# A three-branch mixer in float32 on one core: the next group's key norm, first-group projections and merge gates in other places

## What is computed

```python
def hybrid_mixer(h, w_in, ...):
    p = jnp.einsum('bsd,de->bse', h, w_in)
    u, q, k, v, zr, gl = jnp.split(p, IN_SPLITS, axis=-1)
    y_a = multiscale_pool(u, pool_w, pool_scale)
    y_b = diff_attention(q, k, v, ...)
    y_c = rwkv7_bidir(zr, ...)
    ys = jnp.stack([y_a, y_b, y_c], axis=2)
    branch = jnp.einsum('bsnc,ncd->bsnd', ys, w_branch)
    gates = jax.nn.sigmoid(gl.reshape(b, s, N_BRANCH, D_MODEL) + b_gate)
    merged = jnp.sum(gates * branch, axis=2)
    return jnp.einsum('bsd,de->bse', merged, w_out)

...
    kk = kh * heads(k_k)
    kk = kk / jnp.maximum(jnp.sqrt(jnp.sum(kk * kk, axis=-1, keepdims=True)), 1e-12)
```

## Time and profile before

| | us |
|---|---|
| median of 3 runs | 4690.75 |
| lowest and highest | 4683.18, 4692.92 |
| the profiled execution | 4692.97 |
| its span, first to last instruction | 4691.1 |
| TensorE busy in it | 4439.5 (95%) |
| mean granted clock of TensorE | 0.967 |

### The profile page before, as it was taken

One profiled execution on the slowest core, in us unless ns is written; L12 is line 12 of the kernel. 1 busy time (PEld: TensorE's weight loads), 2 busy tenths in 40 slices (PEclk: granted clock), 3 DMA queues, 4 the chain that ended last, 5 costly groups with the idle time before them and its releaser, 6 DMA issues.

```text
span 4691.1 us, 60760 instructions
## 1 busy us (share of the span) xinstructions
PE 4439.5 (95%) x25140; PEld 2924.7 (62%) x25140; DVE 1411.2 (30%) x3439; ACT 868.6 (19%) x2217; POOL 328.8 (7%) x274
## 2 busy tenths in 40 slices
PE   7999989989998999999998999899999999999999
PEld 3676674434443567675443444587887788788888
DVE  3665550121001556662011000321222331312332
ACT  3123220010000222221001000222222202222220
POOL 0122210000000022120000000000110000011000
PEclk8999989999999999998999999999999999999999
DMA  2001002212221110001221222111111111111111
GB/s 102 33 28 41 32 15 78 84 58 72 76 76 60 53 36 28 33 28 61 81 81 54 76 76 77 45 50 46 55 50 46 50 68 54 48 56 50 51 58 63
DMA packets 71342, 261.60 MB, mean 56 GB/s; under 512 B 7920, under 2 KB 7920, under 8 KB 70816
## 3 DMA queue, kind: packets, MB, share of 16 engines
q1 hardware_dynamic: 69168, 250.62, 15.4%
q10 hardware_dynamic: 1904, 7.11, 0.5%
HBM read 253.51 MB, written 4.19 MB: 55 GB/s over the span
## 4 chain that ended last, share of the span: by engine, by line
PE 88%; DVE 4%; issue 3%; ACT 2%; DVEq 1%; POOLq 0%; DMA 0%; ACTq 0%; SPq 0%
PE ps L2240 26%; PE ps L1422 24%; PE ps L2361 9%; PE ps L1591 4%; PE ps L2326 4%; PE ps L1441 2%; PE ps L1525 2%; PE ps L2270 2%; PE ps L830 1%; PE ps L837 1%; PE ps L796 1%; PE ps L2251 1%; PE ps L822 1%; PE ps L1544 1%; PE ps L2261 1%
## 5 line engine op out<-in xcount | busy, mean ns | idle before, releaser
L2240 PE MATMUL ps<-xT,ring 128*128 128x512 f32 x2656 | 1176.1, 602 | 66.3 <-ACTq L678 47.1
L2240 PEld LDWEIGHTS ps<-xT,ring 128*128 128x128 f32 x2656 | 508.0, 193 | 718.8 <-issue 718.8
L1422 PE MATMUL ps<-xT,ring 128*128 128x264 f32 (+2 forms) x3392 | 800.8, 392 | 17.7 <-DVE arena L1910 10.4
L1422 PEld LDWEIGHTS ps<-xT,ring 128*128 128x128 f32 (+1 forms) x3392 | 643.6, 193 | 138.6 <-DVE arena L1910 13.9
L2361 PE MATMUL ps<-arena,ring 128*128 128x512 f32 x1024 | 440.4, 592 | 2.4 <-ACT arena L2478 1.4
L2361 PEld LDWEIGHTS ps<-arena,ring 128*128 128x128 f32 x1024 | 194.2, 190 | 248.6 <-issue 248.6
L1422 PE MATMUL ps<-arena,ring 128*128 128x264 f32 (+1 forms) x1408 | 320.3, 385 | 2.3 <-DVEq L1811 2.3
L1422 PEld LDWEIGHTS ps<-arena,ring 128*128 128x128 f32 x1408 | 265.9, 191 | 46.4 <-issue 6.1
L1681 ACT ACTIVATE arena<-ps 128x264 f32<-128x264 f32 (+8 forms) x316 | 122.5, 388 | 713.9 <-PE ps L1422 621.6
L1057 ACT ACTIVATE arena<-ps 128x128 f32<-128x128 f32 (+1 forms) x272 | 106.1, 408 | 406.3 <-PE ps L2240 168.0
L2605 DVE TENSOR_TENSOR arena<-arena 128x512 f32<-128x512 f32 x64 | 44.3, 692 | 420.3 <-ACT arena L2478 420.3
(11 more groups left out here) (320 smaller groups left out, 5244.3 us busy)
## 6 DMA issues: line engine op xcount, KB each, us to landing
ring<-in_weights SPq DMA_DIRECT2D x467, 512.0 KB, 3.4
arena<-skew_dram ACTq DMA_DIRECT2D x8, 448.0 KB, 3.1
arena<-in_x SPq DMA_DIRECT2D x1, 2048.0 KB, 10.9
out_rows<-arena SPq DMA_DIRECT2D x8, 256.0 KB, 2.8
skew_dram<-arena ACTq DMA_DIRECT2D x4, 511.5 KB, 5.7
consts<-in_const SPq DMA_DIRECT2D x1, 1384.0 KB, 5.9
consts<-in_const ACTq DMA_DIRECT2D x1, 1252.0 KB, 5.6
arena<-in_buckets SPq DMA_DIRECT2D x1, 127.9 KB, 10.9
```

Source lines behind the costliest of these rows:

```text
L1422: mm = pe.matmul(o[0:m, 0:cols.stop - cols.start], ws[:, k, 0:m], src[:, k, cols], start=k == 0, stop=k == nk - 1)
L2240: m = pe.matmul(o, w[:, k, :], src[:, k, 0:S], start=k == 0, stop=k == KD - 1)
```

## The change

- `norm_keys` of the next group moves on VectorE from ahead of the evacuation of S and Y at step 2 to behind it.
- The u and aq projections of a layer's first group move ahead of `group_pe`: u between the rates and `norm_pe`, aq behind `norm_pe`. ScalarE takes u ahead of the root, and aq behind both `exps`. The lists of tiles follow.
- The merge becomes one loop over eight output blocks, in the same bank lists and counters as the groups. Its first three gate projections stand ahead of `tail_pe` of the last group; behind that, TensorE waits until ScalarE has taken oT. The third branch product of the first block waits for GpSimd's `gated`. ScalarE's three sigmoids stand ahead of `tail_act`. The barrier and the `flush` ahead of the merge, and the end of the counters between its halves, are gone.
- ScalarE's load of constants in the second layer is issued ahead of the sigmoids.

```diff
@@ -577,7 +577,8 @@
         lA = ["low0", "low1", "low2"] + [f"{n}@0" for n in ("zk", "zr", "zv", "w0", "w1", "a0", "a1")]
         lV = ["ssq@0"]
         for c in range(GROUPS):
-            gA = ["u", "vN", "bN0", "kN0", "aq", "bN1", "kN1", "ak", "av"]
+            gA = ["vN", "bN0", "kN0"] + ["aq"] * (c > 0) + ["bN1", "kN1", "ak", "av"]
+            gA = ["u"] + ["aq"] * (c == 0) + gA
             gV = [f"g1{d}{h}{i}" for d in range(2) for i in range(2) for h in range(2)]
             for i in range(2):
                 gV += [f"X1{i}{h}" for h in range(2)] + [f"g20{h}{i}" for h in range(2)]
@@ -601,17 +602,17 @@
...
-        lA += [f"yt@{GROUPS - 1}", f"oT@{GROUPS - 1}"]
+        lA += [f"m0{n}" for n in range(3)] + [f"yt@{GROUPS - 1}", f"oT@{GROUPS - 1}"]
+        lA += [f"m{j}{n}" for j in range(1, KD) for n in range(3)]
+        lV += [f"b{j}{n}" for j in range(KD) for n in range(3)]
-        mrgA = Tiles([f"gate{j}{n}" for j in range(4) for n in range(3)], BA)
-        mrgV = Tiles([f"br{j}{n}" for j in range(4) for n in range(3)], BV)
...
@@ -872,14 +866,16 @@
                     m = pe.matmul(o[:, 0:P], pT[:, b, :], av[:, b, :], start=b == 0, stop=b == 3)
                 a.close(m)
 
-            proj(a, N("u"), ws[c], xT)
+            if c:
+                proj(a, N("u"), ws[c], xT)
             pe.wait_ge(*at("zshift", it, 2))
             turn(a, N("vN"), [rkv[:, 2, n * P:(n + 1) * P] for n in range(4)])
             pe.wait_ge(*at("tilde", it, 0))
             turn_keys(0)
             for i in range(2):
                 gram(1, 0, i)
-            proj(a, N("aq"), ws[c], xT)
+            if c:
+                proj(a, N("aq"), ws[c], xT)
             pe.wait_ge(*at("tilde", it, 1))
             turn_keys(1)
             for i in range(2):
@@ -1066,12 +1062,13 @@
                     act.activation(q[:, m, :], q[:, m, :], ACT.Exp, scale=-1.0, bias=ast[:, z + m:z + m + 1],
                                    accum_out=ast[:, z + 2 + m:z + 3 + m]).then_inc(STEPS["probs"][0], 1)
 
-            take("u", up_[:, 8:8 + S])
+            if c:
+                take("u", up_[:, 8:8 + S])
             take("vN", flat(vN))
             take("bN0", flat(bN[0]))
             take("kN0", flat(kN[0]))
-            take("aq", aq, scale=64 ** -0.5)
             if c:
+                take("aq", aq, scale=64 ** -0.5)
                 squares_o(act)
             take("bN1", flat(bN[1]))
             take("kN1", flat(kN[1]))
@@ -1365,7 +1362,6 @@
                         decay_sums(dve, L, c + 1, 0)
                     if s == 2:
                         decay_sums(dve, L, c + 1, 1)
-                        norm_keys(dve, L, c + 1)
                     if s == 3:
                         keys(dve, L, c + 1)
                 if s < NCH - 1:
@@ -1387,6 +1383,8 @@
                     else:
                         v.close(tt(ysum[:, n, :], ysum[:, n, :], o[:, 0:P], ALU.add))
                 dve.drain()
+                if s == 2 and c < GROUPS - 1:
+                    norm_keys(dve, L, c + 1)
 
         def stack2_pe(pe, first, free, flush):
             ones, i2 = k2("ones"), k2("ident")
@@ -2302,35 +2300,34 @@
                 proj_z(pe, L, 0, a, ws[0], proj)
                 pe.wait_ge(*at("low_ready", L, 2))
                 rates_pe(pe, L, 0, a)
+                proj(a, "u@0", ws[0], xT)
                 norm_pe(pe, L, 0, v)
+                proj(a, "aq@0", ws[0], xT)
                 for c in range(GROUPS):
                     group_pe(pe, L, c, a, v, ws, proj, proj_rows, turn)
+                ws = Slots(w_mrg(L, 0))
+                for j in range(KD):
+                    for n in range(3):
+                        proj(a, f"m{j}{n}", ws, xT)
+                    if j == 0:
+                        tail_pe(pe, L, GROUPS - 1, a, turn)
+                        took(pe, layA, a_pre(L), a_taken, f"oT@{GROUPS - 1}")
+                    w, si = slot(ws)
+                    for n in range(3):
+                        if n == 2:
+                            free(si)
+                            w, si = slot(ws)
+                            if j == 0:
+                                pe.wait_ge(*at("yT_c", L * GROUPS + GROUPS - 1))
+                        o = v.open(f"b{j}{n}")
+                        for k in range(4):
+                            m = pe.matmul(o, w[:, 4 * (n % 2) + k, :], yT[:, 4 * n + k, :], start=k == 0, stop=k == 3)
+                            if k == 0:
+                                first(m)
+                        v.close(m)
+                    free(si)
+                a.end(), v.end()
                 flush()
-                tail_pe(pe, L, GROUPS - 1, a, turn)
-                a.end(), v.end()
-                meet(m_layer(L, 0))
-                for i in range(2):
-                    a = Maker(pe, mrgA, a_mrg(L, i), a_made, a_taken)
-                    v = Maker(pe, mrgV, v_mrg(L, i), v_made, v_taken)
-                    ws = Slots(w_mrg(L, i))
-                    for j in range(4):
-                        for n in range(3):
-                            proj(a, f"gate{j}{n}", ws, xT)
-                        w, si = slot(ws)
-                        for n in range(3):
-                            if n == 2:
-                                free(si)
-                                w, si = slot(ws)
-                            o = v.open(f"br{j}{n}")
-                            for k in range(4):
-                                m = pe.matmul(o, w[:, 4 * (n % 2) + k, :], yT[:, 4 * n + k, :],
-                                              start=k == 0, stop=k == 3)
-                                if k == 0:
-                                    first(m)
-                            v.close(m)
-                        free(si)
-                    a.end(), v.end()
-                    flush()
                 for i in range(2):
                     v = Maker(pe, outV, v_out(L, i), v_made, v_taken)
                     ws = Slots(w_out_(L, i))
@@ -2440,31 +2437,29 @@
                 take_z(act, L, 0, a, "zv")
                 rates_act(act, L, 0, a)
                 keys_act(act, L, 0)
+                o = a.open("u@0")
+                a.close(act.activation(up_[:, 8:8 + S], o, ACT.Copy))
                 root_act(act, L, 0)
                 exps(act, L, 0, 0)
                 exps(act, L, 0, 1)
+                o = a.open("aq@0")
+                a.close(act.activation(aq, o, ACT.Copy, scale=64 ** -0.5))
                 for c in range(GROUPS):
                     group_act(act, L, c, a)
                 squares_o(act)
                 squares_y(act, L, GROUPS - 1)
                 roots_tail(act, L, GROUPS - 1)
-                tail_act(act, L, GROUPS - 1, a)
-                a.end()
-                meet(m_layer(L, 0))
                 if L == LAYERS - 1:
                     act.dma_start(c1[:, K2_AT["prev"][0]:K2_N], const2[:, K2_AT["prev"][0]:K2_N]).then_inc(c2_loaded, 16)
-                act.drain()
-                for i in range(2):
-                    a = Taker(act, mrgA, a_mrg(L, i), a_made, a_taken)
-                    ib = L * 2 + i
-                    for j in range(4):
-                        for n in range(3):
-                            o = a.open(f"gate{j}{n}")
-
-                            act.wait_ge(*before("gates", ib, 3 * j + n))
-                            a.close(act.activation(sg[:, n, :], o, ACT.Sigmoid,
-                                                   bias=lp[:, bass.ds(i * 12 + (LC["bgate"] + 3 * j + n), 1)]))
-                    a.end()
+                for j in range(KD):
+                    for n in range(3):
+                        o = a.open(f"m{j}{n}")
+
+                        act.wait_ge(*before("gates", L * 2 + j // 4, 3 * (j % 4) + n))
+                        a.close(act.activation(sg[:, n, :], o, ACT.Sigmoid, bias=lp[:, LC["bgate"] + 3 * j + n:LC["bgate"] + 3 * j + n + 1]))
+                    if j == 0:
+                        tail_act(act, L, GROUPS - 1, a)
+                a.end()
                 layer_norm(L * 2 + 1, lp[:, LC["ln1g"]:], lp[:, LC["ln1b"]:], v_ln1(L))
                 meet(m_layer(L, 1))
                 if L == LAYERS - 1:
@@ -2568,26 +2563,20 @@
                 tail_mean(dve, L, GROUPS - 1)
                 tail_var(dve, L, GROUPS - 1)
                 tail_recip(dve, L, GROUPS - 1)
-                dve.wait_ge(*at("yT_c", L * GROUPS + GROUPS - 1))
+                for j in range(KD):
+                    for n in range(3):
+                        took(dve, layA, a_pre(L), a_taken, f"m{j}{n}")
+                        o = v.open(f"b{j}{n}")
+                        if n == 0:
+                            v.close(dve.tensor_tensor(mtmp[:, 0, :], o, sg[:, 0, :], ALU.mult))
+                        else:
+                            v.close(dve.tensor_tensor(mtmp[:, 1, :], o, sg[:, n, :], ALU.mult))
+                        dve.drain().then_inc(STEPS["gates"][0], 1)
+                        if n:
```

(21 more changed lines are left out.)

23 lines of the change are left out of this document (9 added, 14 removed).

## The result

The changed kernel takes 4657.66 us (median of 6 runs, 4649.69 to 4657.98) against 4690.06 us of the kernel before (6 runs beside them, 4683.18 to 4694.87): a ratio of 0.9926, 95% interval 0.9915 to 0.9937. The profiled execution took 4657.47 us, with a span of 4655.7 us at a mean granted clock of 0.968, where the one before had 4691.1 us at 0.967. The forecast was 4657.0, range 4624 to 4670.

A forecast was written before the change was run, and what follows sets the result against it. TensorE, 88% of the chain, was taken as the bound, through its waits and half clock. 24.0 + 1.9 + 7.8 + 0.3 = 34.0 us off the profiled 4692.97 gives 4659.0, or 4657 as median; range 4624 to 4670.

The forecast's parts named there:

- Part 1, merge entry: From the last heads_out to the second output block: 33.25 us against 45.25, gaining 12.0 per layer, 24.0 for both.
- The new wait for oT: TensorE at the merge's entry, ahead of the branch products: 1.4 us, costing up to 2 more if the clock falls.
- The third branch product: In the merge's first block, it reads GpSimd's gated product, put at 717.2; the product starts at about 720.
- The middle: At the merge's middle, the pause of 0.95 us per layer goes: 1.9 us for both layers.
- Part 2, key norm: Key norm behind the state's evacuation at step 2: six stretches fall from 142.81 us to 22.5 each, gaining 7.8.
- The wait left at heads_out: TensorE waits there for ScalarE's copy of the transposed probabilities: 2.5 us instead of 4.5 at the state's evacuation.
- a stretch: From L924 at step 3 to the end of the next u projection, six in all: 22.5 us each after.
- the worst case: The clock falls at the wait and stays down: 23.8 us per stretch, gain 0; 1.3 was taken off.
- The 3.3 us that I gave the last stretch: Time at the lower clock in the last of the six, of 20.87 us at clock 0.92; 1.7 us lost.
- Rival (a): The clock holds over the 2.5 us waits: key norm part gives 40.5 us instead of 7.8, total 4624; 15%.
- The stretch at held clock: A stretch after the change if the clock holds: 3.85 + 13.2 = 17.05 us.
- Part 3, head: u and aq in each layer's opening waits: second tilde key 2.0 us sooner at half clock; 0.3 for both layers.

The follow-up runs named there:

- norm_only: Kernel before with only the key norm moved behind the evacuation of the state and of Y at step 2; 4685.57 us, ratio 0.9988.
- head_only: Kernel before with only the u and aq projections of each layer's first group moved ahead of the groups; 4690.35 us, ratio 1.0001.
- merge_only: Kernel before with only the merge's part: gate projections ahead of the last group's tail, no barrier, one loop over eight blocks; 4659.20 us, ratio 0.9930.
- barrier_only: As merge_only against the kernel before, but with the last group's tail still ahead of the three gate projections; 4675.76 us, ratio 0.9968.
- aq_back: Changed kernel with aq of the first group back between its grams, only u staying in the layer's opening; 4658.85 us, ratio 0.9928.
- norm3: Changed kernel with VectorE's key norm one step further back, behind the probabilities' norm of step 3; 4659.16 us, ratio 0.9930.
- early_root: Changed kernel with ScalarE's next-group root and first exponentials in step 2 ahead of zv's eviction, key norm back in its old place; 4605.06 us.
- early_tail: early_root with the turns of yt and oT between the merge's second and third gate projections; 4598.51 us, ratio 0.9803 to the kernel before.
- fill_last: early_tail with the merge's first gate projection ahead of the last group's first step, its sigmoid behind step 0's probabilities; 4587.19 us.

## Why the prediction was right, by its own steps

**Part 1, merge entry: right.** Its parts were 20.6, 0.95, 1.4 and 10.3, together 33.25 us; measured are 20.61, 1.03, 1.15 and 10.41, together 33.20. The new wait for oT is there, 0.25 shorter than said, and it did not pull the clock down (1.00 from 708.64 to 719.05). 24.1 us for both layers against 24.0. The third branch product did not wait for GpSimd. The middle gave 2.4 us against 1.9.

**Part 2, key norm: right in place and in the size of the stretches; what happens outside of them was left out.** The wait left at heads_out was to be 2.5 us and is 2.45, in all six stretches; a stretch was to take 22.5 us and takes 22.9 in the mean when read to the same end as in the earlier trace rows (22.7 to the turns). Against the one trace of before the gain is 5.4 us in the changed kernel and 8.5 in norm_only, where 7.8 was forecast. The sums scatter with the clock, though: before, head_only, merge_only and barrier_only have the same step 3 and sum to 141.8, 136.8, 142.6 and 147.8 us (mean 142.3), after, norm_only, aq_back and norm3 to 136.4, 133.3, 134.8 and 134.8 (mean 134.8). By the means the gain is 7.4 us. The scatter is almost all in each layer's third stretch, which takes 20.7 to 20.8 us in some of the first four kernels and 26.5 in the others. I had taken 1.3 us off the worst case because in some stretches L872 would still run at full clock. Its eight records took 1.13 us in three of the six, 1.73 in one and 2.05 in two, so this holds. One reading of mine was wrong in its words: the 19.97 us in the 23.8 run from L872 at 259.02 to the end of the projection at 278.99, and I took them for a clock that stays down. No run shows a clock that stays down through a u projection: in these 19.97 us the granted clock is 0.63 in the mean, 0.50 up to 268 and 1.00 from 274 on. It comes back inside the u projection, as it does after the change (8.53 us in the first group). The 3.3 us that I gave the last stretch are an estimate that takes its lower level to be the 0.50 of the earlier trace rows. The projection in the first group before:

```profile
270.20 8.79 PE L2240 MATMUL ps<-xT,ring 128*128 128x512 f32 x16
```

At full clock it takes 7.03 us (early_root, granted clock 1.00). The number was the right one to start from, the reason given with it was not.

What I put at nothing is the clock outside of the six stretches. The wait of 2.77 us before the last group's second tilde key left the clock at 1.00 before. After the change it does not, in either layer. TensorE before, then after, first layer:

```profile
589.11 1.09 PE L2261 MATMUL ps<-consts,arena 128*128 128x128 f32 x8 [2.77 <-DVEq L1233]
590.14 2.00 PE L796 MATMUL ps<-arena 64*128 64x256 f32 x16
...
581.76 1.09 PE L2259 MATMUL ps<-consts,arena 128*128 128x128 f32 x8 [2.77 <-DVEq L1230]
582.78 3.52 PE L790 MATMUL ps<-arena 64*128 64x256 f32 x16
```

The grams take 3.52 us for 2.00, at a granted clock of 0.54 for 1.00. The four kernels with the wait of 2.45 us lose 1.3 to 1.6 us there in both layers, the four with the old step 3 lose nothing. The last group's steps, too, take 37.3 to 37.5 us in the former and 36.0 or less in the latter. So what part 2 gives in all is less than its 7.4 us in the stretches; norm_only has 3.5 us by the two traces from the rates to the second block, and 5.1 by the medians. Why the same waits meet another clock there is open.

Rival (a), the full 40.5 us, fell: behind each of the six waits of 2.45 us the granted clock was 0.50 to 0.55 in the 8 us that begin 1 us behind it. It was so behind each wait of this length in the four kernels that have it (24 of 24), and behind most of the waits of 1.40 us in the last group (21 of the 26 in the thirteen kernels that have it, with 0.50 to 0.56 in the same 8 us). The stretch at held clock that I had worked out, 17.05 with its wait, is what early_root and the wait give together (14.46 + 2.45 = 16.91).

**Part 3, head: right that it is worth nothing.** The second key came 2.4 us sooner against 2.0 forecast, behind a wait of 4.11 (forecast over 4), at half clock (0.50 in its transposes). The first key came 0.3 later against 0.6. ak starts 0.14 later in the first layer and 0.26 in the second, where I had 0.15 sooner.

**Sum.** The terms measured are 24.1 + 2.4 + 7.4 - 0.4 = 33.5 us against 34.0 forecast; the medians give 32.4 and the two spans 35.4. With the clock outside of the stretches counted, the pair of traces has 28.5 us for the two layers, each from its rates to the last block's branch products. The other 6.9 us of the spans lie in code that both kernels share, 1.7 of them ahead of the first rates. The part on the merge is right to 0.6 us in 26. That the median came out within 1 us of the forecast is in part luck: single terms scatter by more than that, and what part 2 loses behind its stretches was made up by code that nobody touched.

What I had not seen is the larger thing. I took ScalarE's block of 4.9 us as given and asked only what is late next. It could be moved off step 3 altogether, and then the same stretches take 86.8 us, where they take 134.8 in the mean with the wait of 2.45 us and 142.3 in the mean before.

## What to carry to other kernels

When a wait shrinks and does not go away, ask whose block it was and whether that block can stand in a stretch where nobody wants its engine; moving it past one reader handed the wait to the next here. Price a TensorE wait with the half clock behind it: here a wait of 2.45 us cost 8.3 us, itself included (22.7 us for a stretch of 14.46). And a projection that is put into a wait gains only if the wait's end is what the kernel waits for: at the head, VectorE's chain went on at its own pace, and ak started 0.14 and 0.26 us later.

## What the runs showed of the hardware

Among matmuls of 64 and 128 columns the granted clock fell behind short waits of TensorE: in step 3 behind each of 24 waits of 2.45 us (to 0.50 to 0.55 in the 8 us that begin 1 us behind them) and behind 2 of 6 of 1.63 us (0.54 and 0.50; behind the other four it was 1.00). With the wait gone and the matmuls the same (early_root, early_tail, fill_last) it stayed at 1.00 in all 18 stretches. That need not come out the same each time. The wait of 1.40 us at the last group's first step, windows of 8 us behind it, first and second layer, in the changed kernel and then in early_tail (granted clock third from the right):

```profile
649.60:657.60 8.00, 8.00 (x33) 6.38 (x33) 1.99 (x6) 2.52 (x8) 0.00 (x0) 0.50 0.00 0
2092.97:2100.97 8.00, 8.00 (x33) 6.38 (x33) 2.00 (x6) 2.51 (x8) 0.00 (x0) 0.50 0.00 0
...
625.21:633.21 8.00, 8.00 (x36) 6.83 (x35) 3.31 (x10) 2.24 (x7) 0.00 (x0) 0.54 0.00 0
2041.27:2049.27 8.00, 8.00 (x65) 6.87 (x64) 5.07 (x15) 3.61 (x11) 0.00 (x0) 1.00 0.00 0
```

The same code behind the same wait runs at or near half clock in three of the four and at full clock in one. In the early_tail trace's first layer the clock came back at about 639.5 (0.52 from 625.21 to there, 1.00 from there to 645), among small matmuls and with no projection in between. It had done so in the kernel before as well, at about 670, where eight records of L949 take 1.10 us again (1.00 from 670.3 to 676).

A place that no version touches shows what this does between two traces. Before, and after, in the feed-forward's layer norm behind the same wait of 2.33 us:

```profile
1502.63 8.75 PE L2270 MATMUL ps<-arena,consts 128*128 128x512 f32 x16 [2.33 <-ACT arena L2402]
...
1484.54 7.10 PE L2268 MATMUL ps<-arena,consts 128*128 128x512 f32 x16 [2.33 <-ACT arena L2399]
```

The sixteen records take 8.75 us in the one and 7.10 in the other, at a granted clock of 0.81 and 1.00. The largest such place found is the last group's steps in the second layer, 36.0 us before and 29.5 in merge_only; a ledger of all stretches whose clock can change, and not the difference of two spans, tells what an edit of this size did.
